# Feed-forward blocks 1 to 3: first chunk with channels on partitions, its inverse norm transposed between the two units of chunk 1

## The reference, cut to what matters

```python
def rms_norm(x, w):
    xf = x.astype(jnp.float32)
    y = xf * lax.rsqrt(jnp.mean(xf * xf, axis=-1, keepdims=True) + NORM_EPS)
    return (y * w.astype(jnp.float32)).astype(x.dtype)

def swiglu_ffn(h, w_gate_up, w_down):          # 1024 -> 2 x 2816 -> 1024
    gate, up = jnp.split(h @ w_gate_up, 2, axis=-1)
    return (jax.nn.silu(gate) * up) @ w_down

for layer in range(DEPTH):
    h = h + 0.5 * swiglu_ffn(rms_norm(h, ffn1_norm[layer]), ffn1_w_gate_up[layer], ffn1_w_down[layer])
    ...                                        # the mixer
    h = h + 0.5 * swiglu_ffn(rms_norm(h, ffn2_norm[layer]), ffn2_w_gate_up[layer], ffn2_w_down[layer])
```

## Time and profile before

| | |
|---|---|
| median of three runs | 1028.88 us (1028.53 to 1028.97) |
| profiled execution | 1029.14 us, of which the span is 1027.4 us |
| TensorE clock granted | 0.999 of full speed |
| busy: PE, weight loads, DVE, ACT, POOL | 1016.9, 881.5, 675.4, 569.1, 60.3 us |
| chain that ended last | PE 97%, DVE 1%, ACT 1%, DMA 1% |

### The profile page before, as it was taken

The page is one execution under the profiler, slowest core; times in us unless marked ns, Lnnn a source line. Parts: engine busy times, 40 slices in busy tenths (PEclk is TensorE's granted clock), DMA queues, the critical chain, the costliest instruction groups (busy, mean ns, idle before and its releaser), DMA issues.

```text
span 1027.4 us, 15453 instructions
## 1 busy us (share of the span) xinstructions
PE 1016.9 (99%) x5790; PEld 881.5 (86%) x5790; DVE 675.4 (66%) x1005; ACT 569.1 (55%) x907; POOL 60.3 (6%) x120
## 2 busy tenths in 40 slices
PE   8999999999999999999999999999999999999997
PEld 7888888887888888888888888999999988888886
DVE  5766765576566776635766764688597666776733
ACT  7645543457565654536545543577567655554532
POOL 0000000110000000000000000404205100000000
PEclk9999999999999999999999999999999999999999
DMA  9666465343346555563665465343242347556521
GB/s 322 214 208 200 163 245 201 138 165 109 99 130 228 172 186 216 212 199 102 196 213 191 166 243 205 118 155 123 83 144 83 124 144 231 179 176 219 213 87 41
DMA packets 124308, 175.81 MB, mean 171 GB/s; under 512 B 7360, under 2 KB 97760, under 8 KB 124256
## 3 DMA queue, kind: packets, MB, share of 16 engines
q1 hardware_dynamic: 121552, 172.77, 49.5%
q10 hardware_dynamic: 2704, 2.33, 0.7%
HBM read 174.02 MB, written 1.06 MB: 170 GB/s over the span
## 4 chain that ended last, share of the span: by engine, by line
PE 97%; DVE 1%; ACT 1%; DMA 1%; issue 0%; SPq 0%; ACTq 0%; DVEq 0%
PE bank L1761 29%; PE bank L1691 15%; PE bank L1693 15%; PE bank L1692 14%; PE bank L1763 14%; PE bank L2085 2%; PE bank L2079 2%; PE bank L1988 1%; PE bank L1712 1%; PE bank L1923 1%; PE bank L1954 1%; PE bank L1853 1%; DMA w_raw<-in_ffn_w_gate_up 1%; DVE x_sb L1184 0%; PE bank L2182 0%
## 5 line engine op out<-in xcount | busy, mean ns | idle before, releaser
L1761 PE MATMUL bank<-xT,w_hi 128*128 128x512 f32 x1280 | 444.9, 394 | 0.0
L1147 DVE TENSOR_TENSOR w_lo<-w_raw,w_hi 128x2048 fp32r<-128x2048 f32 x152 | 347.4, 2290 | 105.7 <-ACT w_hi L727 105.0
L727 ACT ACTIVATE w_hi<-w_raw 128x2048 fp32r<-128x2048 f32 x153 | 294.0, 1930 | 118.0 <-PE bank L1693 118.0
L1763 PE MATMUL bank<-xT,w_lo 128*128 128x256 f32 x1280 | 354.8, 277 | 0.0
L1761 PEld LDWEIGHTS bank<-xT,w_hi 128*128 128x128 f32 x1280 | 240.0, 188 | 55.7
L1763 PEld LDWEIGHTS bank<-xT,w_lo 128*128 128x128 f32 x1280 | 240.4, 188 | 0.1
L1691 PE MATMUL bank<-w_hi,hT_hi 128*128 128x512 f32 x352 | 137.5, 391 | 0.0
L1693 PE MATMUL bank<-w_hi,hT_lo 128*128 128x512 f32 x352 | 137.0, 389 | 0.0
L1692 PE MATMUL bank<-w_lo,hT_hi 128*128 128x512 f32 x352 | 137.0, 389 | 0.0
L793 ACT ACTIVATE silu_g<-bank 128x256 f32<-128x256 f32 x80 | 26.4, 382 | 175.4 <-PE bank L1763 175.4
L1234 DVE TENSOR_TENSOR silu_g<-bank,silu_g 128x256 f32<-128x256 f32 x80 | 30.2, 419 | 119.5 <-ACT silu_g L793 119.5
(11 more groups left out here) (312 smaller groups left out, 1218.7 us busy)
## 6 DMA issues: line engine op xcount, KB each, us to landing
w_raw<-in_ffn_w_gate_up SPq DMA_DIRECT2D x170, 512.0 KB, 4.6
w_raw<-in_ffn_w_down SPq DMA_DIRECT2D x88, 512.0 KB, 4.0
w_raw<-in_gdn_w_in SPq DMA_DIRECT2D x32, 512.0 KB, 4.4
w_raw<-in_attn_w_in SPq DMA_DIRECT2D x12, 512.0 KB, 4.1
w_raw<-in_attn_w_out SPq DMA_DIRECT2D x8, 512.0 KB, 3.7
w_raw<-in_gdn_w_out SPq DMA_DIRECT2D x8, 512.0 KB, 3.6
w_raw<-in_ffn_w_gate_up SPq DMA_DIRECT2D x12, 256.0 KB, 6.1
x_sb<-in_x SPq DMA_DIRECT2D x4, 256.0 KB, 5.4
```

The lines of the kernel that those rows point to most:

```text
L727: act.activation(w_hi[u0 % RING][:], w_raw[u0 % RING][:], ACT.Copy).then_inc(hi_ready, 1)
L1147: dve.tensor_tensor(w_lo[u0 % RING][:], w_raw[u0 % RING][:], w_hi[u0 % RING][:].bitcast(F32), ALU.subtract).then_inc(split_ready, 1)
L1761: pe.matmul(banks[m][:], w[0], xT[:, kt, :, :].rearrange("p s n -> p (s n)"), start=(kt == 0), stop=False, skip_group_check=True)
L1763: z = pe.matmul(banks[m][:, SEQ:2 * SEQ], w[1], xT_hi[:, kt, :], start=False, stop=(kt == KT - 1), skip_group_check=True)
```

## The change

Block 0 stays as it was. In blocks 1 to 3 chunk 0 is now computed by `entered_chunk`, which follows the DeltaNet's entry: channels on partitions, `kt` by `kt`, 96 matmuls of 256 columns in place of 48 of 512. The entries of these blocks run by halves (`BY_HALVES`). The four transposes of `h_row` are gone there; the two of `rstd` stay between the units of chunk 1, now into bank 4. The activation, which needs `rstd_rows` now, moves behind these transposes: ACT copies the rows, DVE multiplies the gate half by them, ACT takes the Silu, DVE multiplies by the up half, ACT and DVE write `hT_hi` and `hT_lo`. ACT's and DVE's splits of units u + 4 and u + 5 come ahead of all this. The DeltaNet's two matmuls on `rstd` become two transposes. Banks are dealt out anew.

```diff
+BY_HALVES = {2: 0, 3: 1, 4: 2, 5: 3}
...
+        ENTER_BANKS = {0: (4, 6), 1: (4, 2)}
+        FIRST_CHUNK = (2, 3)
+        CHUNKS = [(2, 3, 4, 5), (6, 7, 0, 1)]
+        ROWS_BANK = 4
...
 # ACT
-                        elif e == E_GDN and n < 2 and j == 1:
+                        elif e in BY_HALVES and n < 2 and j == 1:
                             z.then_inc(early_hi, 1)
...
                 root(RSTD_FFN[f])
-                act.wait_ge(rstd_ready, RSTD_FFN[f])
-                first_chunk(f)
-                if f == 0:
+                if f:
+                    split_hi(u + 4)
+                    split_hi(u + 5)
+                    copy_rows(ROWS_FFN[f], ROWS_BANK)
+                    act.wait_ge(g_scaled, NCH * f)
+                    act.activation(silu_g[0][:], silu_g[0][:], ACT.Silu).then_inc(g_silu, 1)
+                    act.wait_ge(h_cols, NCH * f)
+                    act.activation(hT_hi[:, 0:BANK], h_row[0][:].rearrange("p m n -> p (m n)"),
+                                   ACT.Copy).then_inc(hT_hi_ready, 1)
+                else:
...
 # DVE
-                if e == E_GDN:
+                if e in BY_HALVES:
                     for n in range(2):
                         residual(e, n, factor)
...
+                if f:
+                    split_lo(u + 4)
+                    split_lo(u + 5)
+                    dve.wait_ge(rows_ready, ROWS_FFN[f])
+                    dve.wait_ge(unit_done, u + 2)
+                    dve.tensor_tensor(silu_g[0][:], bank[FIRST_CHUNK[0]][:].rearrange("p (m n) -> p m n", m=2),
+                                      rstd_rows[:].rearrange("p t n -> p (t n)").unsqueeze(1).broadcast_to([P, 2, SEQ]),
+                                      ALU.mult).then_inc(g_scaled, 1)
+                    dve.wait_ge(g_silu, NCH * f)
+                    dve.scalar_tensor_tensor(h_row[0][:], bank[FIRST_CHUNK[1]][:].rearrange("p (m n) -> p m n", m=2), 0.5,
+                                             silu_g[0][:], ALU.mult, ALU.mult).then_inc(h_cols, 1)
+                    dve.wait_ge(hT_hi_ready, NCH * f + 1)
+                    dve.tensor_tensor(hT_lo[:, 0:BANK], h_row[0][:].rearrange("p m n -> p (m n)"),
+                                      hT_hi[:, 0:BANK].bitcast(F32), ALU.subtract).then_inc(hT_lo_ready, 1)
...
 # PE
                     if j == 1 and kh == 0 and not looped(i):
-                        first_transposes(f)
+                        if f:
+                            transposed_rstd(RSTD_FFN[f], ROWS_BANK)
+                        else:
+                            first_transposes()
...
+            def transposed_rstd(n, b):
+
+                pe.wait_ge(rstd_ready, n)
+                for t in range(TT):
+                    z = pe.transpose(bank[b][:, t * P:(t + 1) * P], rstd[:, t:t + 1].broadcast_to([P, P]), ident[:])
+                z.then_inc(rows_psum, 1)
+
+            def entered_chunk(f):
+
+                e, u = E_FFN[f], U_FFN[f]
+                for kh in range(2):
+                    wait_split(pe, u + kh)
+                    for q in range(4):
+                        if q < 3:
+                            pe.wait_ge(early_lo, 6 * BY_HALVES[e] + 3 * kh + q + 1)
+                        else:
+                            pe.wait_ge(xT_lo_ready, 4 * e + 2 * kh + 2)
+                        kt = 4 * kh + q
+                        for m in range(4):
+                            z = products(bank[FIRST_CHUNK[m // 2]][:, m % 2 * SEQ:(m % 2 + 1) * SEQ],
+                                         ring(u + kh, slice(q * BANK + m * P, q * BANK + (m + 1) * P)),
+                                         (xT_hi[:, kt, :], xT_lo[:, kt, :]),
+                                         start=(kt == 0 and m % 2 == 0), stop=(kt == KT - 1), skip_group_check=True)
+                        if q == 3:
+                            z.then_inc(unit_done, 1)
+                        elif kh == 0 and q < 2:
+                            enter(e, 2 + q)
...
             def ffn(f, e_next):
-                for kh in range(2):
-                    in_unit(U_FFN[f] + kh, 0, kh, FIRST_CHUNK[f], E_FFN[f])
-                if f == 0:
+                if f:
+                    entered_chunk(f)
+                else:
+                    for kh in range(2):
+                        in_unit(kh, 0, kh, FIRST_CHUNK, E_FFN[0])
...
-            def rstd_in_rows():
-
-                pe.wait_ge(rstd_ready, RSTD_GDN)
-                for t in range(TT):
-                    z = pe.matmul(bank[7][:, t * P:(t + 1) * P], rstd[:, t:t + 1].broadcast_to([P, P]), ident[:],
-                                  start=True, stop=True)
-                z.then_inc(rows_psum, 1)
...
                     if kh and j == 3:
-                        rstd_in_rows()
+                        transposed_rstd(RSTD_GDN, 7)
```

More of the change, by code:

```diff
@@ L296, in enter_bank, with chunk_banks @@
                 return bank[FIRST_BANKS[j]][:, 0:P]
+            if e in E_FFN[1:]:
+                return bank[((4, 5), (acc_of(e)[0][0], acc_of(e)[1][0]), (4, 4), (5, 5))[n][j // 2]][:, j * P:(j + 1) * P]
             return bank[ENTER_BANKS[e][t] + half][:, j * P:(j + 1) * P]
-        def chunk_banks(f, j):
-            return [bank[b] for b in CHUNKS[f][0 if j % 2 else 1]]
+        def chunk_banks(j):
+            return [bank[b] for b in CHUNKS[j % 2]]
         raw_loaded = [sem(f"raw_loaded{i}") for i in range(RING)]
@@ L827, in two_chunks @@
                 def two_chunks(i):
-                    if not looped(i):
-                        first_hT_hi(f)
+                    if f == 0 and not looped(i):
+                        first_hT_hi()
                     gate_chunk(f, 1, i)
@@ L944, in _ @@
             root(RSTD_GDN)
-            act.wait_ge(rows_psum, ROWS_GDN)
-            act.activation(rstd_rows[:], bank[7][:, 0:TT * P].rearrange("p (t n) -> p t n", t=TT),
-                           ACT.Copy).then_inc(rows_ready, 1)
+            copy_rows(ROWS_GDN, 7)
             act.wait_ge(wba_zero, 1)
@@ L1288, in ffn @@
                 dve.wait_ge(rstd_ready, RSTD_FFN[f])
-                first_chunk(f)
+                if f:
[13 more added lines that the diff above has]
+                else:
+                    first_chunk()
                 def two_chunks(i):
-                    if not looped(i):
-                        first_hT_lo(f)
+                    if f == 0 and not looped(i):
+                        first_hT_lo()
                     gate_chunk(f, 1, i)
@@ L1757, in gate_chunk, with channel_step @@
                             wait_split(pe, u0)
+                        z = channel_step(u0, 4 * kh + q, banks)
+                    z.then_inc(unit_done, 1)
+                    if j == 1 and kh == 0 and not looped(i):
+                        if f:
+                            transposed_rstd(RSTD_FFN[f], ROWS_BANK)
+                        else:
+                            first_transposes()
+            def channel_step(u0, kt, banks):
+                for m in range(4):
+                    w = ring(u0, slice(kt % 4 * BANK + m * P, kt % 4 * BANK + (m + 1) * P))
+                    pe.matmul(banks[m][:], w[0], xT[:, kt, :, :].rearrange("p s n -> p (s n)"),
+                              start=(kt == 0), stop=False, skip_group_check=True)
+                    z = pe.matmul(banks[m][:, SEQ:2 * SEQ], w[1], xT_hi[:, kt, :], start=False,
+                                  stop=(kt == KT - 1), skip_group_check=True)
+                return z
@@ L1758, in gate_chunk @@
                         kt = 4 * kh + q
                         for m in range(4):
-                            w = ring(u0, slice(q * BANK + m * P, q * BANK + (m + 1) * P))
-                            pe.matmul(banks[m][:], w[0], xT[:, kt, :, :].rearrange("p s n -> p (s n)"),
-                                      start=(kt == 0), stop=False, skip_group_check=True)
-                            z = pe.matmul(banks[m][:, SEQ:2 * SEQ], w[1], xT_hi[:, kt, :], start=False,
-                                          stop=(kt == KT - 1), skip_group_check=True)
```

91 lines of the change are left out of this document (43 added, 48 removed).

## The result

The kernel after takes 1033.52 us (median of five runs, 1033.28 to 1035.53), the kernel before 1028.59 us beside it (five runs, 1028.48 to 1028.97). The ratio is 1.0049, 95% interval 1.0037 to 1.006: slower by 4.9 us, where I had forecast 1027.9 us and a range up to 1030.0. Each step that the prediction priced went as priced. The loss is in a part of the kernel that the prediction did not price at all.

The account below looks back on a forecast made before the run. PE was taken to bound the kernel, read as distances between starts. Terms of +0.55, -1.32 and -0.22 us gave -0.99 us, from the median of 1028.88 to 1027.9 us, with a range of 1026.9 to 1030.0 us.

Parts of the forecast that it names:

- Term 1: Entry and chunk 0, blocks 1 to 3: 96 matmuls of 256 columns for 48 of 512, together +0.55 us.
- Term 2: Chunk 1 of blocks 1 to 3: four transposes of `h_row` removed in each, 0.44 us a block, -1.32 us.
- Term 3: DeltaNet: two float32 matmuls on `rstd`, 0.44 us, become two transposes, 0.22 us; -0.22 us.
- The chain: From `rstd`'s transposes to chunk 2, blocks 1 to 3: `hT_lo` ready 0.6 to 0.7 us early, no stall, no cost.
- Rival (a): Ahead of chunk 2: `hT_lo` comes late through ACT's table load, PE stands; 1028.5 to 1029.9 us; chance 14%.
- Rival (b): Entries of blocks 1 to 3: DVE's splits come late, PE waits 0.6 us a block; 1029.8 us; chance 6%.
- Rival (c): Chunk 0, blocks 1 to 3: 256-column matmuls take half the time of 512s, 0.115 us; 1026.5 us; chance 6%.

Follow-up runs that it names:

- behind123: The changed kernel with 1, 2 and 3 unused identity transposes added behind rstd's two in blocks 1, 2 and 3; 1032.04 us, one execution.
- nudge: The changed kernel with one unused identity transpose behind the first four matmul pairs of chunk 1's first unit, blocks 1 to 3; 1027.74 us, ratio 0.9993.

## Why the prediction was wrong

- **Term 1, entry and chunk 0**: right. 12.65 us in each block against a forecast of 12.64; +0.58 us over the three blocks against +0.55.
- **Term 2, transposes of `h_row`**: right in what it names, 0.43 us a block against 0.44, and wrong in what it leaves out. This is the step that failed. It let the four transposes save their own time, and let everything behind them stand. They were also what ended the long pace: without them the 304 pairs behind `rstd`'s transposes, which the sum took at no change, keep it in each block, +2.02 us a block, +6.05 us in all, more than four times what the term saved.
- **Term 3, `rstd` in the DeltaNet**: right, -0.23 us against -0.22.
- **The chain, taken at nothing**: right, with 1.0 us of room, of which 0.10 us comes from the long pace itself. Rival (a) is out: the load started beside the multiplication and nothing follows it. By the Trainium skill, "ScalarE: Activation LUTs", on what ACT_TABLE_LOAD costs, a drain of 1.38 us would come with it; the row of the Silu, 0.01 us behind the load's end, shows none behind the load, and the load began 0.01 us behind the end of ACT's copy, so none ahead of it either.
- **Rival (b)**: out, the first product follows after 0.24 us. **Rival (c)**: out, a 256-column matmul takes 0.12 us from start to start. The gap by which the prediction gave (c) its 1026.8 us (the Trainium skill, "TensorE: Matmul & The Clock Gate", on the back-to-back issue gap) stands there as that of an isolated matmul, not of one in a stream, which the prediction did not say; with 230 and 120 ns measured, rival (c) fails without it.
- **The range and the chances**: I gave 4% to what I did not see, either way. The sum had +0.55, -1.32 and -0.22 us in it and 1280 pairs of matmuls with no term, because their code was unchanged; a change of 2% in their pace is more than all three terms. The evidence was in the earlier trace rows, where I used 5.63 us for the chain and did not set it against the 5.64 us of a first unit, which has no slow first matmul in it.

## What to carry to other kernels

In a kernel that is one dense stream of matmuls, work out the mean distance between starts for every stretch, in the kernel before too: if two stretches of the same instructions differ, find out what lies between them before taking it away. Give unchanged loops a term in the sum, their count times the spread of paces seen, since a few instructions removed at their head can change all of them. After a change, compare starts over the same number of matmuls; PE's busy share and the clock were the same here, and its waits differed by 0.2 us.

## What the runs showed of the hardware that I had not expected

- The same sequence of matmuls (512 and 256 columns in turn, full clock, nothing waited for) ran at 346.7 or 353.3 ns a pair, and kept the one or the other for 304 pairs and more.
- Transposes in the stream can turn the pace either way: six behind the long pace turned it short in all four blocks of before, six behind the short pace made it long in block 0 of behind123. One stretch of 304 pairs is worth 2.0 us, 0.2% of this kernel.
- The same instructions can go either way, within one execution (nudge: blocks 1 and 2 short, block 3 long) and from one kernel to another where no edit touches them (block 0: short in after, long in behind123). That two executions of one kernel differ so is argued from times alone: two of the fifteen runs of before beside nudge took 1030.32 us, 1.8 over their median, and nudge has three such runs of eleven, one of them with a trace.
